# w_out of the FFNs by seven block products for two groups of eight gated rows

## The reference

```
def swiglu(x, w_in, w_out):
    a, b = jnp.split(x @ w_in, 2, axis=-1)
    return (jax.nn.silu(a) * b) @ w_out
...
    for l in range(DEPTH):
        h = h + 0.5 * swiglu(rmsnorm(h, ffn1_norm[l]), ffn1_w_in[l], ffn1_w_out[l])
        u = rmsnorm(h, mix_norm[l])
...
        h = h + merged @ w_out[l]
        h = h + 0.5 * swiglu(rmsnorm(h, ffn2_norm[l]), ffn2_w_in[l], ffn2_w_out[l])
    return rmsnorm(h, final_norm)
```

## Time and profile before

| | |
|---|---|
| time, median of 3 runs (lowest to highest) | 2153.89 us (2153.53 to 2153.96) |
| the profiled execution: its own time, its span | 2153.99 us, 2152.2 us |
| mean granted TensorE clock | 0.998 of full speed |
| busy share of the span: PE, PEld, DVE, ACT, POOL | 99%, 87%, 64%, 41%, 64% |
| one FFN on TensorE (4 S, 18 K, w_out) | 43.5 + 181.4 + 119.7 us |
| transfers | 210.81 MB, mean 98 GB/s |

### The profile page before, as it was taken

One profiled execution on the slowest core, in us unless ns is written; L12 is line 12 of the kernel. 1 busy time (PEld: TensorE's weight loads), 2 busy tenths in 40 slices (PEclk: granted clock), 3 DMA queues, 4 the chain that ended last, 5 costly groups with the idle time before them and its releaser, 6 DMA issues.

```text
span 2152.2 us, 36180 instructions
## 1 busy us (share of the span) xinstructions
PE 2130.2 (99%) x12838; PEld 1881.5 (87%) x12838; DVE 1373.7 (64%) x2582; ACT 882.2 (41%) x1717; POOL 1380.6 (64%) x1030
## 2 busy tenths in 40 slices
PE   9999999999999999999999999999999999999997
PEld 7998998878888899899889899888888888998996
DVE  6763886578754577177568448746877456752863
ACT  5532532544553354054145235225445533531541
POOL 6776778644446667587667667785444374876773
PEclk9999999999999999999999999999999999999999
DMA  5343333222213223333333433342122132333332
GB/s 171 107 156 97 106 96 122 96 69 65 74 54 103 98 89 99 98 104 99 107 101 118 133 98 104 101 130 79 64 74 69 48 119 79 104 101 95 115 95 82
DMA packets 90028, 210.81 MB, mean 98 GB/s; under 512 B 9824, under 2 KB 13064, under 8 KB 89608
## 3 DMA queue, kind: packets, MB, share of 16 engines
q1 hardware_dynamic: 85680, 203.32, 29.5%
q10 hardware_dynamic: 4184, 5.31, 0.8%
HBM read 206.48 MB, written 3.68 MB: 98 GB/s over the span
## 4 chain that ended last, share of the span: by engine, by line
PE 92%; DVE 5%; ACT 2%; issue 1%; DMA 0%; ACTq 0%; DVEq 0%; SPq 0%
PE bank L869 17%; PE bank L870 17%; PE bank L871 17%; PE bank L1005 11%; PE bank L1007 11%; PE bank L1006 11%; PE tbank L1222 1%; DVE mem L2040 1%; DVE yL L2048 1%; DVE bank L2015 1%; ACT u1H L1554 1%; DVE h L2020 1%; PE obank L1268 0%; DVE ssq L2023 0%; DVE bank L2030 0%
## 5 line engine op out<-in xcount | busy, mean ns | idle before, releaser
L741 POOL TENSOR_TENSOR wL<-raw,wH 128x1024 fp32r<-128x1024 f32 (+3 forms) x280 | 548.8, 1960 | 23.4
L738 POOL TENSOR_SCALAR wH<-raw 128x1024 fp32r<-128x1024 f32 (+3 forms) x280 | 248.3, 887 | 487.5 <-PE bank L871 421.0
L1005 PE MATMUL bank<-u1H,wH 128*128 128x256 f32 x1152 | 326.4, 283 | 3.3 <-DVE hidL L1940 3.3
L1006 PE MATMUL bank<-u1H,wL 128*128 128x256 f32 x1152 | 326.0, 283 | 0.0
L1007 PE MATMUL bank<-u1L,wH 128*128 128x256 f32 x1152 | 326.0, 283 | 0.0
L869 PE MATMUL bank<-u1H,wH 128*128 128x512 f32 x704 | 281.6, 400 | 0.0
L870 PE MATMUL bank<-u1H,wL 128*128 128x512 f32 x704 | 274.9, 391 | 0.0
L871 PE MATMUL bank<-u1L,wH 128*128 128x512 f32 x704 | 274.8, 390 | 0.0
L869 PE MATMUL bank<-hidH,wH 128*128 128x512 f32 x704 | 274.4, 390 | 0.0
L870 PE MATMUL bank<-hidH,wL 128*128 128x512 f32 x704 | 274.0, 389 | 0.0
L871 PE MATMUL bank<-hidL,wH 128*128 128x512 f32 x704 | 273.9, 389 | 0.0
(11 more groups left out here) (291 smaller groups left out, 4731.9 us busy)
## 6 DMA issues: line engine op xcount, KB each, us to landing
raw<-in_wA SPq DMA_DIRECT2D x296, 256.0 KB, 3.1
raw<-in_wM SPq DMA_DIRECT2D x96, 512.0 KB, 3.3
raw<-in_wB SPq DMA_DIRECT2D x64, 384.0 KB, 3.1
raw<-in_wB SPq DMA_DIRECT2D x64, 320.0 KB, 2.9
raw<-in_wA SPq DMA_DIRECT2D x28, 512.0 KB, 3.3
raw<-in_wR SPq DMA_DIRECT2D x32, 256.0 KB, 2.6
mem<-in_memT SPq DMA_DIRECT2D x2, 1024.0 KB, 7.9
near_bias<-bias_rows ACTq DMA_DIRECT2D x2, 1024.0 KB, 6.6
```

The costliest lines, as they stand in the source:

```text
L738: pool.tensor_scalar(wH[:, w, 0:cols], raw[:, slot, 0:cols], 1.0, 0.0, ALU.mult, ALU.add).then_inc(rounded, 1)
L741: pool.tensor_tensor(wL[:, w, 0:cols], raw[:, slot, 0:cols], wH[:, w, 0:cols].bitcast(F32), ALU.subtract).then_inc(split_done, 1)
L1005: pe.matmul(dst, a, hi, start=begin and k == 0, stop=False)
L1006: pe.matmul(dst, b, hi, start=False, stop=False)
```

## The change

The two parts and their two `outs` go. One sequence `FLOW` per FFN has 22 hidden pairs and 8 pairs of a new kind "O". The hidden rows form groups A and B of eight and C of six. For A and B, w_out is made by four "O" pairs each: the same seven products, with a pair of output rows of `h` in place of a and b and the group's eight gated rows in place of the eight input rows. Only C goes through `outs()` at the end, with one 768-column weight unit per output row instead of two.

The block sums of gated rows that this needs are made per couple of a near row (at < 4) and a far row (at >= 4): DVE makes one 256-column sum when the near row is finished and three when the far one is (`couple_sums`, in `window()` between `sum_four(then)` and `mix_first(now)`), ACT rounds them (`couple_highs`), POOL makes their low parts (`couple_lows`). Gated rows of A and B are written to an SBUF tile `keep` instead of staying in bank 3, and `low` reads them there. Rows of C are multiplied by `rms` in the gate, so that `outs()` can add straight to the scale of `h`; an "O" pair is multiplied by `rms` when it is finished. `add_rows` adds an "O" pair to `h`.

The memory's mean square is made in pieces in the windows after "O" pairs (`square_mem`, `add_mem`; two loads of 512 KB into `keep`); its norm and split (`norm_mem`, `low_mem`) stand behind the first and the second row of the end of the FFN. `outs()` makes rows 0 and 1 up to the last hidden row and then finishes both. ACT's loop at the end is written out, with waits on constants.

```diff
-HALF = (12, 10)
-PATTERN = ("SSSS" + 8 * "K", 10 * "K")
+GROUPS = {"A": (0, 8), "B": (8, 8), "C": (16, 6)}
+COUPLES = (0, 4, 1, 5, 2, 6, 3, 7)
...
+    order = [("S", "A", t) for t in COUPLES[:4]] + [("K", "A", t) for t in COUPLES[4:]]
+    order += [("K", "C", 0)] + [("O", "A", i) for i in range(4)]
+    order += [("K", "B", t) for t in COUPLES] + [("K", "C", 1)] + [("O", "B", i) for i in range(4)]
+    order += [("K", "C", t) for t in range(2, N_OUT)]
...
-MEM_MEAN_AT = 3
+MEM_MEAN_AT = 1
...
+            near4H, near4L = sb("near4H", [P, 4, TH], F32R, ffn), sb("near4L", [P, 4, TH], F32R, ffn)
+            far4H, far4L = sb("far4H", [P, 4, T], F32R, ffn), sb("far4L", [P, 4, T], F32R, ffn)
+            sumH = sb("sumH", [P, KD, T], F32R, ffn)
+                sumS = sb("sumS", [P, KD, T], F32, unrounded)
+            sumL = sb("sumL", [P, KD, T], F32R, ffn)
+                keep = sb("keep", [P, 2, T], F32, within)
...
+                            if f == 0 and (p.group, p.at) == ("C", 4):
+                                sp.wait_ge(product_done, 7 * k_at(l, f, pair_of("O", "B", 3)) + 7)
+                                sp.dma_start(mem[:, :, :], memT).then_inc(mem_loaded, 16)
...
+                            if f == 0 and p.at == 2:
+                                load_mem_piece(p.group)
...
+                def couple_lows(f, p):
+                    c, j = couple_at(ffn_at(l, f), p), p.at % 4
+                    for i, r in enumerate((2 * j + 1, 2 * j)):
+                        pool.wait_ge(couple_sum, 4 * c + 4)
+                        pool.wait_ge(couple_high, 2 * c + i + 1)
+                        pool.tensor_tensor(sumL[:, r, :], sumS[:, r, :], sumH[:, r, :].bitcast(F32), ALU.subtract
+                                           ).then_inc(couple_low, 1)
...
+                            k_weights(f, p)
+                        before = FLOW[p.pos - 2] if p.pos >= 2 else None
+                        if before is not None and in_couple(before) and before.at >= 4:
+                            couple_lows(f, before)
...
+                            take_unit(u + i)
+                            if i < 2:
+                                rows(i, range(N_OUT - 1))
                             else:
+                                rows(i, range(N_OUT)).then_inc(unit_used, 1)
+                            if i == 1:
+                                for first in range(2):
+                                    rows(first, (N_OUT - 1,)).then_inc(unit_used, 1)
...
-                        dve.tensor_tensor(bank[3][:, 0:TH], bank[3][:, 0:TH], sg[:, 1, TH:T], ALU.add)
+                        own.done(dve.tensor_tensor(bank[3][:, 0:TH], bank[3][:, 0:TH], sg[:, 1, TH:T], ALU.add))
                         own.wait()
...
+                    def add_rows(p):
+                        own.done(dve.tensor_tensor(bank[3][:, :], bank[3][:, :], rms[:, :], ALU.mult))
+                        own.wait()
+                        for i, made in ((0, obank), (1, bank[3])):
+                            row = h[:, 2 * p.at + i, :]
+                            own.done(dve.scalar_tensor_tensor(row, made[:, :], 0.5, row, ALU.mult, ALU.add))
+                        own.wait()
+                        dve.sem_inc(pair_done, 1)
...
+                            if p.group == "C":
+                                own.done(dve.tensor_tensor(bank[3][:, :], bank[3][:, :], rms[:, :], ALU.mult))
+                                own.wait()
...
-                            dve.tensor_tensor(bank[3][:, :], bank[3][:, :], sg[:, 0, :], ALU.mult).then_inc(k_gated, 1)
+                            dve.tensor_tensor(dst, bank[3][:, :], sg[:, 0, :], ALU.mult).then_inc(k_gated, 1)
...
+                        src = (bank[3] if p.group == "C" else kept(p))[:, 0:hi.shape[-1]]
-                            dve.tensor_tensor(hidL[:, p.pos, :], bank[3][:, :], hidH[:, p.pos, :].bitcast(F32),
-                                              ALU.subtract).then_inc(pair_done, 1)
+                            dve.tensor_tensor(lo, src, hi.bitcast(F32), ALU.subtract).then_inc(pair_done, 1)
...
+                        if p.at < 4:
+                            dve.tensor_tensor(sumS[:, 2 * j, left], keep[:, 0, right], keep[:, 0, left], ALU.subtract
+                                              ).then_inc(couple_sum, 1)
+                            return
+                        dve.tensor_tensor(sumS[:, 2 * j + 1, right], keep[:, 1, right], keep[:, 0, right], ALU.subtract
+                                          ).then_inc(couple_sum, 1)
+                        dve.tensor_tensor(sumS[:, 2 * j + 1, left], keep[:, 1, right], sumS[:, 2 * j, left], ALU.subtract
+                                          ).then_inc(couple_sum, 1)
+                        dve.wait_ge(couple_sum, 4 * c + 3)
+                        dve.tensor_tensor(sumS[:, 2 * j, right], keep[:, 1, left], sumS[:, 2 * j + 1, left], ALU.subtract
+                                          ).then_inc(couple_sum, 1)
...
+                        if last is not None and in_couple(last):
+                            couple_sums(last)
...
-                last_half(0, 8, G_MIX, u1H, u1L)
+                for k in range(KD):
+                    last_row(k, 0, 8, G_MIX, u1H, u1L)
+                    if k == 0:
+                        norm_mem()
+                    if k == 1:
+                        low_mem()
```

More of the change, by code:

```diff
@@ L42 @@
 RAW_SLOTS, SPLIT_SLOTS, BANKS = 2, 4, 4
-HALF = (12, 10)
 TH = T // 2
-PATTERN = ("SSSS" + 8 * "K", 10 * "K")
-Pair = namedtuple("Pair", "kind n pos unit chunk run")
+GROUPS = {"A": (0, 8), "B": (8, 8), "C": (16, 6)}
+COUPLES = (0, 4, 1, 5, 2, 6, 3, 7)
+N_OUT = GROUPS["C"][1]
+Pair = namedtuple("Pair", "kind n hid pos unit chunk run group at")
 def lay_pairs():
[L55 to L72, removed]
@@ new lines, in lay_pairs, with pair_of, in_couple, couple_at @@
+    return flow, count["S"], count["7"], hid, unit
+FLOW, N_S, N_K, N_HID, OUT_UNIT = lay_pairs()
+OUT_CHUNK = OUT_UNIT
+U_FFN = C_FFN = OUT_UNIT + KD
+N_GROUP = {"A": 0, "B": 1}
+assert N_K % 2 == 0 and U_FFN % 4 == 0
+def pair_of(kind, group, at):
+    return next(p for p in FLOW if p.group == group and p.at == at and (p.kind == "O") == (kind == "O"))
+def in_couple(p):
+    return p.kind != "O" and p.group in "AB"
+def couple_at(ffn, p):
+    return ffn * 8 + N_GROUP[p.group] * 4 + p.at % 4
@@ L699, in layer @@
+                    for q in ("A11", "A12", "A21", "A22"):
+                        quarters_free(q, last_k(l, f))
+                    units(wC, 16, KD * f, KD, N_OUT * P, unit + OUT_UNIT)
                 ffn_units(0)
@@ L1021, in seven_products @@
+                    def seven_products(p):
                         g = k_at(l, f, p)
                         low, high = slice(0, TH), slice(TH, T)
-                        bank_free(part, p, 0)
+                        bank_free(p, 0)
                         pe.wait_ge(pool_low, pool_lows_to(g, "A11"))
-                        product(bank[0][:, low], g, "A11", lambda k: row(k, 0), begin=True, end=True)
-                        bank_free(part, p, 1)
+                        if p.kind == "O" and p.at == 0:
+                            pe.wait_ge(pair_done, k_at(l, f, pair_of("K", p.group, 7)) + 1)
+                        product(bank[0][:, low], g, "A11", lambda k: row(p, k, 0), begin=True, end=True)
+                        bank_free(p, 1)
@@ L1027, in seven_products @@
                         pe.wait_ge(pool_low, pool_lows_to(g, "A12"))
-                        product(bank[1][:, low], g, "A12", lambda k: row(4 + k, 0), begin=True)
+                        product(bank[1][:, low], g, "A12", lambda k: row(p, 4 + k, 0), begin=True)
                         if p.run == 0:
@@ L1082, in _ @@
+                    for p in FLOW:
+                        if p.kind == "S":
+                            standard(p)
+                        else:
+                            seven_products(p)
+                    outs()
                 ffn(0, 0, 8, 1)
@@ L1951, in window @@
-                        if k_now:
+                            if last.kind == "O":
+                                add_rows(last)
+                            else:
+                                gate(last)
+                        if seven_now:
                             low_late(now, "A22")
-                        if last is not None:
+                        if last is not None and last.kind != "O":
                             low(last)
-                        if k_now:
+                        if seven_now:
@@ L1984, in ffn @@
                     own.restart()
[L1985 to L2007 removed]
+                    hidden()
                     own.done(dve.memset(ssq[:, :], 0.0))
```

509 lines of the change are left out of this document (258 added, 251 removed).

## The result

The changed kernel takes 2288.94 us in the median (2282.87 to 2295.40, four runs) against 2153.93 before: 1.0627 times as long, 95% interval 1.0598 to 1.0657. The forecast was 2216, with a range up to 2262: the sign was right, the size wrong by 73 us.

The account below looks back on a forecast made before the run. The prediction took TensorE, busy 99% of the span, as the bound: matmul count times pitch. Its terms, -25.8 + 52 + 34 + 3 - 0.7 = +62.5 on 2153.99, gave 2216 us, with an 8-in-10 range of 2155 to 2262.

Parts of the forecast that it names:

- TensorE's work, -25.8: Matmul time in all FFNs: w_out matmuls removed against "O" pairs and group C added, 6.4 us less per FFN.
- VectorE in the windows, +52: Seven-product windows: VectorE operations with two SBUF inputs wait for GpSimd, 13.0 us per FFN, +52 in all (0 to 91).
- 9.36 a window when late: VectorE's round in a seven-product window, once its 0.33 wait for the sigmoid goes: 9.36 us of 10.08.
- 1.41 per couple: VectorE's added work in a couple's two windows without blocking: 1.41 us against 1.44 of room, so no cost.
- the layout by hand, 2.2 of blocking per couple: VectorE's low parts and sums placed against GpSimd's instructions in a couple's two windows: 2.2 us blocked, between 0 and 3.3.
- the sums fit in that gap, 0: The far row's three sums, directly behind `sum_four`, precede GpSimd's last low part and lose 0 us.
- the memory's additions: `add_mem` in "O" windows of a layer's first FFN: 0.34 us or more of VectorE work, no cost in time.
- The upper bound: Most blocking per couple in the windows: six instructions at the mean excess of L2040, 3.3 us.
- The end of the first FFN, +34: From `outs` to w_in in each layer's first FFN: X+62 against 45.1 undisturbed, 17 us lost per layer, +34.
- The other ends, +3 - 0.7: End of layer 0: slower rows and late joint release, +3 us (0 to 4); very end: one multiply less, -0.7.
- The first: Rival: TensorE stays the bound throughout, VectorE's sums unblocked in the windows; 2128 us, chance 0.09.
- The third: Rival: GpSimd becomes the bound in the windows, 31 us per FFN in place of 13; 2288 us, chance 0.2.

Follow-up runs that it names:

- e7: Changed kernel, whole computation: gated rows kept and read in PSUM banks, couple sums ahead of `sum_two`, memory's sums on GpSimd; 2162.33 us, ratio 1.0037.
- e8: e7 with the memory's norm and low parts dealt out over gaps between output rows, and its inverse rms in PSUM; 2150.87 us, ratio 0.9982.
- e13: Changed kernel with one edit: the memory's eight additions (`add_mem`) moved from VectorE to GpSimd; 2273.57 us, ratio 1.0552.
- e4: Changed kernel with 18 added matmuls, results unused, ahead of TensorE's long waits for `mixed` to keep its clock up; 2272.59 us, ratio 1.0546.
- e9: e8 with the memory's chain (mean, root, norm, low parts) begun one output row earlier; 2143.29 us, ratio 0.9945.
- e5: Changed kernel with low parts and couple sums reading one PSUM input (other numbers), and memory's additions on GpSimd; 2165.89 us, ratio 1.0051.
- e10: Changed kernel with couple sums ahead of `sum_two` and `sum_four`, still with two SBUF operands, and memory's additions on GpSimd; 2210.32 us, ratio 1.0257.

## Why the prediction was wrong

**TensorE's work, -25.8: right.** The pitches are unchanged (10.08 a window in e7, 8.2 us for 36 matmuls of 512), and e7 and e8 show windows without a wait.

**VectorE in the windows, +52: wrong, measured some +134.** The 26 windows of the four FFNs took 297.4, 294.3, 300.0 and 294.2 us, against 262.1 each: 137.5, less the 3.3 of before. Of VectorE's own sum the parts without blocking held: 9.36 a window when late, 1.41 per couple. The term that failed is the layout by hand, 2.2 of blocking per couple, and in it "the sums fit in that gap, 0". By the rows above, with 0.41, 0.42 and 0.69 as unblocked durations, the far row's low lost 0.64 (forecast 0.7), its three sums 0.56 + 0 + 1.11 = 1.67 (0), the near row's low 1.02 (0.6), its sum 0.57 (0.9): 3.90. Then 2 x 9.36 + 1.41 + 3.90 = 24.03, and the 24.3 measured has 0.3 more, the wait for `near4H`, which ScalarE makes behind a rounding that waits for TensorE. The gap was not empty in the rows that the forecast used. The earlier trace rows have GpSimd's low part of S3 from 251.53 to 252.83, over the place at 252.10 that the forecast gave the first sum; it looked only at the low part of S1, at 253.43. `sum_two` of that window is this row:

```profile
250.66 0.70 DVE L1851 TENSOR_TENSOR sbank<-tbank,wS 128x512 f32<-128x512 f32 x1 [0.79 <-issue]
```

From its start to those two low parts it is 0.87 and 2.77 us there, and 0.84 and 2.75 in the window of B1 after the change; most other windows of the two traces have the same. In the second case GpSimd is idle until `sum_two` comes, so however late VectorE is, its sums find the low part of S3 beside them. I had that wait in the code and did not lay it out. The first sum's loss of 0.56 then pushes the third one onto the low part of S1: without it the three sums (1.14 us from 949.06) would have ended at about 950.2, ahead of 950.38. This last step is an estimate; no run has the first sum alone unblocked. Why the near row's low part lost 1.02 and not 0.6 I did not trace.

The rest is made up of four things, in us per FFN: the 1.7 more of blocking in six couples, 10; the memory's additions, 4 on the mean of the four ("nothing" in the forecast; 15.4 us by e13); the clock, 4 by e4, most of it in the first windows of the "O" runs, which the forecast did not have; some 2 that I did not separate. With the 13 forecast that is about 33, against 134 / 4 = 33.5. The two middle terms are differences of medians; by the windows of the profiled executions each is nearer 6, and then the parts add up to a little more than was lost. They are known no better than that.

**The upper bound.** 3.3 per couple "by the mean of L2040" was no bound: 3.90 is beyond it. A mean from a stage with other spans of GpSimd (L2040's 908 ns) says nothing on the worst case; L2040's longest, 1785 ns, in the same rows, would have.

**The end of the first FFN, +34: right.** X + 62 was forecast, 60.7 measured, 15.6 a layer more than 45.1. (The forecast's own steps, X + 55.9, 3.6 and 3.4, add up to X + 62.9.) Inside, the low parts were quicker than taken (476 ns in the mean, not 958) and the norm slower.

**The other ends, +3 - 0.7: nearly right.** From the last matmul of the second FFN's `outs()` to the 24th of the next FFN it is 15.0 us against 10.9, so 4.1 where 3 was taken (0 to 4). From the last matmul of the last `outs()` to the span's end it is 14.8 us against 15.6.

Together -25.8 + 134 + 31 + 4 - 1 = 142, against 141.4 measured.

**The rivals.** The first (TensorE the bound, 2128) is what e7 to e9 come near to once the operands are changed. The third gave 2288, the time that came, for another reason: GpSimd is not the bound. It idles 1.07 and 0.63 us for VectorE and ScalarE in the rows above, and in e5, with 16 instructions more, the windows are 10.1. The number agreed, the mechanism did not.

The Trainium skill, page "SBUF — State Buffer", section "Who interferes with whom", was the right rule, cited for the right instructions: whichever of the two starts first keeps the other out for a whole instruction. The rows agree: 1.52 us for 0.41 of work behind a GpSimd instruction of 1.26 started 0.02 us before. Which of them starts first is set by the order of this kernel, and that decided the size.

## What to carry to other kernels

Before new instructions go into an order, lay every instruction of the other engine over their place, not only the last one, and carry each delay on to the next instruction: the sums were put beside a low part of 1.30 us that stood in the rows, and its delay brought a second one. Lay out the waits too: here GpSimd waits for VectorE, so the two meet at the same distance in every window, early or late. Before an order is fixed, look for the idle time ahead of a waiting instruction (0.79 us here) and put the new, independent work in front of that wait; this alone gave back 63 of 135 us. The idle time stood in the trace of the kernel before (0.79 ahead of L1851). Where VectorE and GpSimd are both busy, leave a value in PSUM as long as VectorE still reads it, so that no VectorE operation has two SBUF inputs. The two remedies overlap: e7, with the changed kernel's whole work, lies 127 us below it with both and the memory's sums on GpSimd. Of these the operands are worth 48 on top of the rest (e10 to e7). Once the operands are in PSUM, the order is worth little: e5 has the old one, and PSUM operands of other numbers, and lies only 4 us above e7.

## What was unexpected in the hardware

TensorE's granted clock fell behind rather short waits. In the windows of the changed kernel 22 of the 24 waits of 2.05 to 3.06 us were followed by 12 to 27 matmuls at the 1.2 GHz level (1.6 us longer with 16), the two others, of 2.41 and 2.81, by none; in e10 two waits of 1.80 and 1.77 us, ahead of 230 and 1299 us, were followed by 17 each. The loss mattered mostly where TensorE itself was the bound (e4: some 330 of 430 slow matmuls gone, 16 us won). The exclusion works both ways: GpSimd's L848 took 1.61 us at 945.78, with VectorE's two-input low started at 944.90, against 1.30 in the earlier trace rows; in e10 it took 1.75 at 917.62, behind a low part started at 916.44.
